# Scan stage of a mixer: three-pass projections, one shared weight ring, rotation tables made ahead

## The reference, cut to what matters

```python
u = rmsnorm(x, mix_norm)
proj = u @ w_in
u_ssm, q, k, v, xq, g_ssm, g_attn, g_mem = jnp.split(proj, cuts, axis=-1)
y_ssm = gelu(s5_scan(u_ssm, ...))          # x_t = Abar x_{t-1} + Bbar u_t, complex, per state
br_ssm = glu_a * sigmoid(glu_b)            # of y_ssm @ ssm_w_glu
br_attn = dilated_mixture_attention(q, k, v, rel_table) @ attn_w_up
br_mem = memory_cross_attention(xq, ...) @ xattn_w_up
merged = sigmoid(g_ssm) * br_ssm + sigmoid(g_attn) * br_attn + sigmoid(g_mem) * br_mem
x = x + merged @ w_out
```

## Time and profile before

| | |
|---|---|
| median of 3 runs (lowest to highest) | 3720.09 us (3719.6 to 3721.9) |
| span of the profiled execution, first to last instruction | 3716.1 us |
| the profiled execution's own total | not recorded apart from its span |
| TensorE busy | 3560.3 us, 96% of the span |
| VectorE, ScalarE, GpSimd busy | 1736.3, 1300.6, 442.0 us |
| scan stage, from its first instruction to the last one of its gelu | 2683.3 to 2956.2 us |
| first and last product of the gates | 2731.7 and 2951.4 us |
| first product of the heads stage | 2964.5 us |
| TensorE's granted clock over the span | 0.979 |

### The profile page before, as it was taken

The page is one execution under the profiler, slowest core; times in us unless marked ns, Lnnn a source line. Parts: engine busy times, 40 slices in busy tenths (PEclk is TensorE's granted clock), DMA queues, the critical chain, the costliest instruction groups (busy, mean ns, idle before and its releaser), DMA issues. The chain is left out here.

```text
span 3716.1 us, 50584 instructions
## 1 busy us (share of the span) xinstructions
PE 3560.3 (96%) x20104; PEld 2915.6 (78%) x20104; DVE 1736.3 (47%) x2492; ACT 1300.6 (35%) x1796; POOL 442.0 (12%) x468
## 2 busy tenths in 40 slices
PE   8999799799999999989999999999999899899998
PEld 7999777699999999755547888888744477678886
DVE  5442466544434443266625443543377633545433
ACT  4332366433323332134524332433110143324421
POOL 0000222100000000011006400000144233330000
PEclk9999899899999999989999999999999999999999
DMA  4322321022222222300013223222212331233222
GB/s 171 133 88 86 121 57 52 21 89 90 83 86 103 90 87 78 137 23 26 1 37 111 102 81 107 94 102 85 102 52 82 113 89 57 95 121 113 90 86 83
DMA packets 116604, 318.07 MB, mean 86 GB/s; under 512 B 13863, under 2 KB 57127, under 8 KB 100484
## 3 DMA queue, kind: packets, MB, share of 16 engines
q1 hardware_dynamic: 116484, 316.51, 25.3%
HBM read 307.98 MB, written 17.01 MB: 87 GB/s over the span
## 5 line engine op out<-in xcount | busy, mean ns | idle before, releaser
L347 PE MATMUL acc<-fb_xh,fb_wh 128*128 128x264 f32 x1408 | 286.6, 285 | 3.2 <-DVE fb_wl L507 3.2
L347 PE MATMUL acc<-fb_xh,fb_wl 128*128 128x264 f32 x1408 | 287.8, 286 | 0.0
L347 PE MATMUL acc<-fb_xl,fb_wh 128*128 128x264 f32 x1408 | 286.9, 285 | 0.0
L347 PE MATMUL acc<-fd_xh,fd_wh 128*128 128x512 f32 x704 | 275.5, 391 | 3.2 <-DVE fd_wl L507 3.2
L347 PE MATMUL acc<-fd_xh,fd_wl 128*128 128x512 f32 x704 | 274.4, 390 | 0.0
L347 PE MATMUL acc<-fd_xl,fd_wh 128*128 128x512 f32 x704 | 274.4, 390 | 0.0
L422 ACT ACTIVATE fb_wh<-fb_raw 128x2048 fp32r<-128x2048 f32 (+1 forms) x74 | 124.7, 1685 | 286.1 <-PE acc L406 173.8
L347 PEld LDWEIGHTS acc<-fb_xh,fb_wh 128*128 128x128 f32 x1408 | 220.3, 189 | 3.6 <-DVE fb_wl L507 3.5
L347 PEld LDWEIGHTS acc<-fb_xh,fb_wl 128*128 128x128 f32 x1408 | 219.0, 189 | 0.0
L347 PEld LDWEIGHTS acc<-fb_xl,fb_wh 128*128 128x128 f32 x1408 | 218.4, 189 | 0.0
L502 DVE TENSOR_TENSOR fb_wl<-fb_raw,fb_wh 128x2048 fp32r<-128x2048 f32 (+1 forms) x74 | 148.3, 2004 | 141.4 <-ACT fb_wh L422 140.6
(11 more groups left out here) (542 smaller groups left out, 8754.7 us busy)
## 6 DMA issues: line engine op xcount, KB each, us to landing
fb_raw<-wi_dram SPq DMA_DIRECT2D x42, 1024.0 KB, 4.8
fd_raw<-wi_dram SPq DMA_DIRECT2D x42, 1024.0 KB, 4.8
fb_raw<-wo_dram SPq DMA_DIRECT2D x32, 704.0 KB, 4.1
fd_raw<-wo_dram SPq DMA_DIRECT2D x32, 704.0 KB, 4.1
fa_raw<-wi_dram SPq DMA_DIRECT2D x20, 1024.0 KB, 4.8
ff_raw<-wi_dram SPq DMA_DIRECT2D x20, 1024.0 KB, 4.8
a_raw<-a_qkv_dram SPq DMA_DIRECT2D x24, 512.0 KB, 4.2
s_gw<-gate_w_dram SPq DMA_DIRECT2D x24, 512.0 KB, 3.9
```

The lines of the kernel that those rows point to most:

```text
L347: last = pe.matmul(acc[:, up_base(p, b) + 2 * a + q, 0:w], x[:, k, a, :], part[:, k, t0:t0 + w], start=k == 0 and part is xh and x is wv, ...
```

## The change

What it does:

* `m_xn`, its rounded part and its rests (`m_xh`, `m_xl`) and one ring of four weight chunks (`m_raw`, `m_wh`, `m_wl`) now belong to the mixer and serve the scan and the heads stage. ScalarE rounds, GpSimd makes the weights' rests, VectorE the rests of x, as in the heads stage before.
* The four chunks of `u` and the 24 gates are made in three passes of rounded numbers. Two gates (`EARLY = 2`) come before the loop, the other 22 in it.
* The scan stage also loads and splits the first three weight chunks of the heads stage (`READY = 3`).
* GpSimd combines `coarse` and `fine` to the full rotation tables during the FFN stage, in 64 pieces of 128x256, and stores each with a DMA of its own queue to DRAM, waiting for each store before it makes the next (`store_turns`). In the loop SyncE loads a step's table (512 KB) into one of two buffers, once the step two before has been rotated.
* The gelu moves to the start of the heads stage. Three gates are held instead of four.

```diff
-        GATES_HELD = 4
+        GATES_HELD = 3
...
                         if ahead:
                             ahead.work(pool)
+                            pool.wait_ge(split, piece_done(0, 0))
+                            ahead.store_turns(pool)
...
+            def store_turns(self, pool):
...
+                            if done:
+                                pool.wait_ge(turns_stored, 16 * done)
+                            pool.tensor_tensor(to, slow(0), fast(x), ALU.mult)
+                            pool.tensor_tensor(t, slow(1), fast(y), ALU.mult)
+                            pool.drain()
+                            pool.tensor_tensor(to, to, t, op)
+                            pool.drain()
...
+                            pool.dma_start(turn_dram[s, r][:, cols], first_w[:, 0:HALF * self.FINE]
+                                           ).then_inc(turns_stored, 16)
...
-            EARLY = 0
+            EARLY = 2
+            U = 4
+            NW, RING = U + GATES + READY, MIX_RING
...
+                    def load_turns(s):
+                        sp.dma_start(turns[:, s % 2, :, :], turn_dram[s].rearrange("r p n -> p r n")
+                                     ).then_inc(turn_there[s % 2], 16)
...
+                        if n in step_of_last and step_of_last[n] + 2 < SC:
+                            sp.wait_ge(rotated, 1 + step_of_last[n] + 1)
+                            load_turns(step_of_last[n] + 2)
...
+                    for j in range(RING, NW):
+                        sp.wait_ge(split, 1 + j - RING + 1)
+                        weights(j)
+                        if j >= U + 7:
+                            store_gate(j - U - 7)
...
+                    for j in range(NW):
+                        pool.wait_ge(rounded, 1 + j + 1)
+                        pool.tensor_tensor(wl[:, j % RING, :], raw[:, j % RING, :],
+                                           wh[:, j % RING, :].bitcast(F32), ALU.subtract).then_inc(split, 1)
                     arm(pool, "d_")
...
+                    def product(j, to, first=False):
+                        pe.wait_ge(split, 1 + j + 1)
                         for k in range(KC):
...
+                            if first:
+                                pe.wait_ge(x_lo, 1 + k + 1)
+                            ks = slice(k * P, (k + 1) * P)
+                            for x, part_ in ((wh, xh), (wh, xl), (wl, xh)):
+                                last = pe.matmul(to, x[:, j % RING, ks], part_[:, k, :],
+                                                 start=k == 0 and x is wh and part_ is xh,
+                                                 stop=k == KC - 1 and x is wl)
+                        last.then_inc(chunk_mm, 1)
...
+                    round_weights(0)
+                    for k in range(KC):
+                        act.wait_ge(normed, 1 + k + 1)
+                        act.activation(xh[:, k, :], xn[:, k, :], ACT.Copy).then_inc(x_hi, 1)
+                    for j in range(1, RING):
+                        round_weights(j)
+                    for c in range(U):
+                        act.wait_ge(chunk_mm, 1 + c + 1)
                         act.activation(u[:, c, :], acc[:, c, :], ACT.Copy).then_inc(u_ready, 1)
+                        round_weights(c + RING)
...
-                    for c in range(4):
-                        act.wait_ge(y_pre, 1 + c + 1)
-                        act.activation(yg[:, c, :], yg[:, c, :], ACT.Gelu_apprx_tanh)
...
-                        dve.wait_ge(spun, 1 + s + 1)
+                        dve.wait_ge(turn_there[s % 2], 1 + 16 * (s // 2 + 1))
...
+                        if last_chunk(j) >= READY:
+                            pe.wait_ge(split, split_done(last_chunk(j)))
...
-                    for k in range(4):
-                        act.activation(xh[:, k, :], xn[:, k, :], ACT.Copy).then_inc(x_hi, 1)
-                    round_weights(0)
-                    for k in range(4, KC):
-                        act.activation(xh[:, k, :], xn[:, k, :], ACT.Copy).then_inc(x_hi, 1)
-                    for j in range(1, RING):
+                    for c in range(4):
+                        act.activation(yg[:, c, :], yg[:, c, :], ACT.Gelu_apprx_tanh)
+                    for j in range(READY, RING):
                         round_weights(j)
```

More of the change, by code:

```diff
@@ L1862, in work, with slow, fast, scan_stage @@
                         unit()
-        def scan_stage(st, xn, yg, tables):
-            FINE, COARSE, fine, coarse = tables.FINE, tables.COARSE, tables.fine, tables.coarse
+            def store_turns(self, pool):
+                HALF = self.COARSE // 2
+                to, t = (first_w[:, n * HALF * self.FINE:(n + 1) * HALF * self.FINE].rearrange(
+                    "p (a b) -> p a b", a=HALF) for n in range(2))
+                done = 0
+                for s in range(SC):
+                    for r, x, y, op in ((0, 0, 1, ALU.subtract), (1, 1, 0, ALU.add)):
+                        for half in range(2):
+                            rows = slice(half * HALF, (half + 1) * HALF)
+                            def slow(c):
+                                return self.coarse[:, c, s, rows].unsqueeze(2).to_broadcast([P, HALF, self.FINE])
+                            def fast(c):
+                                return self.fine[:, c, s, :].unsqueeze(1).to_broadcast([P, HALF, self.FINE])
+                            if done:
[5 more added lines that the diff above has]
+                            pool.drain()
+                            cols = slice(half * HALF * self.FINE, (half + 1) * HALF * self.FINE)
+                            pool.dma_start(turn_dram[s, r][:, cols], first_w[:, 0:HALF * self.FINE]
+                                           ).then_inc(turns_stored, 16)
+                            done += 1
+                pool.wait_ge(turns_stored, 16 * done)
+        def scan_stage(st, xn, xh, xl, ring, yg, tables):
             mag, sin_, cos_ = (tables.v[:, n, :] for n in (tables.MAG, tables.SIN, tables.COS))
@@ L2269, in weights @@
                                          ).then_inc(there[j % RING], 16)
-                    for j in range(RING):
+                    for j in range(READY, READY + RING):
                         weights(j)
@@ L2281, in _ @@
                     sp.dma_start(mem, mem_t).then_inc(c_mem, 16)
-                    for j in range(RING, len(chunks)):
-                        sp.wait_ge(split, 1 + j - RING + 1)
+                    for j in range(READY + RING, len(chunks)):
+                        sp.wait_ge(split, split_done(j - RING))
                         weights(j)
@@ L2287, in _ @@
                 def _(pool):
-                    for j in range(len(chunks)):
-                        pool.wait_ge(rounded, 1 + j + 1)
+                    for j in range(READY, len(chunks)):
+                        pool.wait_ge(rounded, 1 + j - READY + 1)
                         pool.tensor_tensor(wl[:, j % RING, :], raw[:, j % RING, :],
@@ L2319, in unit @@
                         else:
-                            last = product(at_chunk[(kind, n)], acc[:, b, :], xh, xl, first=j == 0)
+                            last = product(at_chunk[(kind, n)], acc[:, b, :], xh, xl)
                         last.then_inc(proj_mm, 1)
```

170 lines of the change are left out of this document (80 added, 90 removed).

## The result

| | before | changed |
|---|---|---|
| median of 4 runs each, taken together | 3720.27 us (3719.6 to 3721.9) | 3676.44 us (3674.83 to 3679.11) |
| ratio, 95% interval | | 0.988 (0.9867 to 0.9892) |
| total of the profiled execution, its span | not recorded, 3716.1 us | 3679.11, 3677.2 us |
| TensorE busy | 3560.3 us | 3528.3 us |
| GpSimd busy | 442.0 us | 597.2 us |

What follows compares the result with a forecast made beforehand. TensorE was taken to bound the scan stage. Span 3716.1 - 45.3 (loop) + 12.8 (front) - 12.0 (end) + 1.0 (FFN stage) = 3672.6 us, as a median 3676.6; range 3664 to 3694.

Steps and rivals of the forecast that it cites:

- The loop, -45.3: Scan loop: 22 gates at 5.44 us plus projections and inputs, 177.3 us on TensorE instead of 222.6, 45.3 less.
- The front, +12.8: Scan stage from the norm to the loop: chunks and two early gates start the loop at 2743.9, 12.8 us later.
- The lower bound that the prediction gave: Front: loop start at 2739.7 without lock, cold clock and rounding, instead of 2743.9.
- The end, -12.0: Change from scan to heads stage: x and three chunks are ready, 6.7 us instead of 18.7, 12.0 less.
- The FFN stage, +1.0: FFN stage: 64 table pieces at 6.7 us are hidden with 150 us to spare; 1.0 us on the path.
- Rival 1: FFN stage: GpSimd does not finish the tables; a piece takes 10.0 us, total 3738; chance 0.07.
- Behind the change, 0: Rest of the heads stage and output projection: no term in the prediction, entered as 0.
- Rival 2: Scan loop: tables or gates come late, loop 192 us instead of 177, total 3691; chance 0.12.
- Rival 3: Front: the lock with GpSimd delays VectorE's constants, B and C ready only about 2745, total 3688; chance 0.10.
- The rule of ports: VectorE operations with two SBUF inputs and GpSimd operations reading SBUF exclude each other; loop not slowed, otherwise 60 us longer.
- the 4.0 us that I added to the span: Whole program: the median of the runs lies 4.0 us above the profiled span, added to the forecast span at the end.

Runs made afterwards that it cites:

- The two runs above: Two runs against the changed kernel: no heads-stage weights loaded in the scan stage (READY = 0), 3685.16 us; gelu back at the end of the scan stage, 3679.97 us.

## Why the prediction was right, and where it wasn't

* **The loop, -45.3: -43.4 measured.** The reason holds: the sum of TensorE's list bounds it (177.3 by the sum, 178.6 measured, 0.8 idle), and the passes were the cause, by the run without them. The difference lies on both sides of the subtraction: the old loop came out 222.0 and not at the 222.6 of the window, the new one 1.3 above its sum, where the first pass of a gate takes 0.34 us and I had 0.227. That VectorE's sum was 2% below was right and mattered more than I made of it: with one pass less, or two gates less, the loop is 177.4 or 176.3. Traffic in the loop was 123 GB/s and not 156. Of the 43.8 us, 35.4 are gone without the three passes. By the stage table, the run without them is still 10.1 us shorter than before: 11.9 of the end and 13.7 of the loop, less 15.4 of the front and 0.2 behind.
* **The front, +12.8: +8.5 measured; the term that was mis-sized.** I added 2.35 to the norm for one lock of GpSimd. Its subtraction fell for the most part beside the reciprocal and held up one multiplication by 0.6 us; the 16 operations ended 11.1 us after the first one began, where I had 11.0 and the lock on top. I added 1.0 for the cold clock, but it was back before chunk 0 ended, and chunk 0 waited for x anyway. Chunk 1 began 2.7 us behind the norm and not 3.4, as its rounding began before VectorE was through. The rest, about 0.4, was saved between the last early gate and the loop. The lower bound that the prediction gave for all three additions gone, 2739.7, is what came out on that scale (2683.3 + 56.3 = 2739.6).
* **The end, -12.0: -11.9 measured.** Unit 0 runs at full clock, and its first copy comes 7.5 us after the last projection. The two runs above divide it.
* **The FFN stage, +1.0: 0.0.** The store was priced from the wrong neighbour, at 3.9; it took 2.0. A piece took 5.6 us against 6.7, so 221 us were to spare and not 150. Rival 1 needed 9.04. No lock reached the path.
* **Behind the change, 0: +2.5.** Not in the prediction; it is the clock, see below.
* **Rival 2** (tables late in the loop): VectorE waited 3.1 us for tables. My account had about 3 us of waits too, but for TensorE. A third buffer gained nothing, and without early gates VectorE waited 10.4 us for tables and the loop was no longer than its two gates more. Where GpSimd made the tables behind its subtractions and with two buffers, it came true, at 24.8 us.
* **Rival 3** (the lock holds the constants): the lock acted as it said, on the operations that it named, and was covered by about 5 us. With no early gates TensorE waited 4.9 us for C; with tables made beside it, 8.3.
* **The rule of ports** (the Trainium skill, SBUF — State Buffer, section "SBUF: two separate sides"): both halves are seen. Operations of VectorE with an operand in PSUM took 0.68 to 0.70 us in the loop, beside 49.7 us of GpSimd and also beside 136.4; those with two operands in SBUF waited whole operations of GpSimd out. But the rule as the prediction gave it is too narrow: a `TENSOR_SCALAR` of 128x16 (L2118), which reads one tensor, took 2.27 us among the others of 2.3. And the prediction counted 27 subtractions in the loop, where there are 21; the loss if each had blocked an operation was 49 us and not 60.

The total was right to 0.2 us, better than its terms: the front was priced 4.3 too high and the FFN stage 1.0, the gain of the loop 1.9 too high, and 2.5 behind the change were missing. That they nearly cancel is luck, and so is the last digit; each is small against the range that I gave. Of the 4.0 us that I added to the span, 1.9 lie around it in the changed kernel's profiled execution (3679.11 - 3677.2); if it was the same before, the profile that I read was of an execution some 2 us quicker than the median.

## What to carry to other kernels

Write out each engine's sum for a loop before and after: here TensorE's fell from 224.9 to 177.3 and stopped 2% above VectorE's 173.8, so taking away one more pass, or two more gates, shortened the loop by only 1.2 and 2.3 us. To move a gate from the loop to its front gains only where TensorE would else wait in the front. And what an engine does late depends on what stands ahead in its list: the same tables cost 24.8 us in the loop in one order, and nothing in the other, or with one buffer more. Two-operand work in SBUF on VectorE is best placed where GpSimd has pauses, and short idle times of TensorE are best kept short, since the clock fell behind some of them.

## What the runs showed of the hardware that I had not expected

**The same code behind the same gap doesn't always get the same clock.** In the heads stage TensorE is nearly idle for 3 us. These are the windows of that gap and of the 10 us behind it, in the kernel before, the changed one, and the one without early gates; the code there is the same:

```profile
3081.60:3084.60 3.00, 0.54 (x5) 0.55 (x6) 2.38 (x3) 2.39 (x5) 3.00 (x2) 1.00 0.01 3
3084.60:3094.60 10.00, 10.00 (x47) 7.42 (x45) 4.30 (x10) 3.33 (x6) 1.62 (x1) 0.83 0.33 104
```

```profile
3040.30:3043.30 3.00, 0.55 (x5) 0.56 (x6) 2.39 (x3) 2.37 (x5) 3.00 (x2) 0.99 0.06 5
3043.30:3053.30 10.00, 10.00 (x35) 7.29 (x34) 3.57 (x9) 2.44 (x4) 1.61 (x1) 0.66 0.33 103
```

```profile
3045.40:3048.40 3.00, 0.52 (x5) 0.52 (x6) 2.36 (x3) 2.41 (x5) 3.00 (x2) 1.00 0.00 1
3048.40:3058.40 10.00, 10.00 (x60) 7.74 (x60) 4.32 (x10) 4.35 (x7) 2.41 (x2) 1.00 0.33 104
```

After one and the same gap the granted clock averaged 0.83, 0.66 and 1.00, with 47, 35 and 60 matmuls done in the same 10 us. Over the whole stretch from the first unit of the heads to the end of the output projection, I summed TensorE's busy time times the share of the clock that was missing, in steps of 1 us: 5.1 us before, 8.5 in the changed kernel, 6.6 without early gates. Idle time was 23.3, 22.3 and 21.8. The stretch took 365.1, 367.6 and 365.1. In all 14 profiles those with 6.8 or less took 364.3 to 366.1, those with 8.5 to 8.9 took 367.0 to 367.6. So the 2.5 us that the change lost behind itself are clock (+3.4) less idle time (-1.0), to 0.1 us, and are no work. Why the clock differs is not shown.

**The same is the spread between executions.** Up to the first product of `fd_` all 14 kernels have the same instructions; that point came between 1957.7 and 1966.6 us. The same sum over that stretch, in steps of 2 us, was 35.4 us in the kernel before (1959.4), 40.7 in the changed one (1965.0), 35.7 in the earliest and 42.1 in the latest. The idle time was 95.6 to 97.9 in all. So a difference of up to 7 us between two single profiles of this kernel can be clock alone.

**A stop of 1.1 us kept the clock, one of 2.7 us didn't**, at the same place of the program: 0.23 us from pass to pass from the first microsecond on in the changed kernel, 0.43 for 3.4 us with the gelu before the barrier. One pair shows no threshold: the gap of 3 us above kept it in one run of three. And the stop of 1.1 us doesn't bring the clock back: with two passes, where the last projection already ran at half clock, the passes behind the same stop followed each other by 0.43 us.
